# Attention mixers of a hybrid block: sparse-attention steps taken in pairs, and three work lists merged by how an item uses the TensorE array

## What is computed

```python
def dsa_mixer(q, k, v, q_idx, k_idx, w_idx, rel_bias_dsa):   # 4 heads of 64, one shared k and v
    def block(inp):                                          # 128 queries at a time
        ...
        _, sel = lax.top_k(score, n_sel)                     # done in an earlier stage, as a mask
        logits = jnp.einsum('bthd,btkd->bhtk', qb, kg).astype(f32)
        logits = jnp.where(valid[:, None], logits + bias, -jnp.inf)
        probs = jax.nn.softmax(logits, axis=-1).astype(vg.dtype)
        return jnp.einsum('bhtk,btkd->bthd', probs, vg)

def swa_mixer(q, k, v, sinks, rel_bias_swa):                 # 8 heads, window of 128
    logits = jnp.einsum('bnqhgd,bnkhd->bnhgqk', qb, kw).astype(f32) + bias.astype(f32)
    ...
    out = jnp.einsum('bnhgqk,bnkhd->bnqhgd', probs.astype(vw.dtype), vw)

def gla_mixer(q, k, v, g, a_lr, w_alpha2, b_alpha, g_norm):  # gated linear attention, chunks of 64
    def step(state, inp):
        o = o_inter + jnp.einsum('bhts,bhsv->bhtv', scores, vi)
        state = (jnp.exp(b_last[:, :, 0, :])[..., None] * state
                 + jnp.einsum('bhsk,bhsv->bhkv', ki * jnp.exp(b_last - bi), vi))
```

## Time and profile before

| what | value |
|---|---|
| three runs | 2830.13, 2831.82, 2831.91 us |
| median | 2831.82 us |
| profiled execution, span from first to last instruction | 2830.9 us |
| outside the span, against the median | 0.9 us |
| mixers: first instruction after the stage's start, last copy out issued | about 845 us, 1357.15 us |
| mixers, PE / DVE / ACT busy in 845 to 1357 us | 441.9 / 393.3 / 343.2 of 512 us |

### The profile page before, as it was taken

The page is one execution under the profiler, slowest core; times in us unless marked ns, Lnnn a source line. Parts: engine busy times, 40 slices in busy tenths (PEclk is TensorE's granted clock), DMA queues, the critical chain, the costliest instruction groups (busy, mean ns, idle before and its releaser), DMA issues. The chain is left out here.

```text
span 2830.9 us, 34992 instructions
## 1 busy us (share of the span) xinstructions
PE 2596.2 (92%) x10908; PEld 1642.9 (58%) x10909; DVE 1813.7 (64%) x2566; ACT 1283.1 (45%) x2400; POOL 922.8 (33%) x925
## 2 busy tenths in 40 slices
PE   6988779999987899898799979999999999998998
PEld 3634323344863445444688756666666666665787
DVE  2176999699977788876333486644644444743676
ACT  2277867967956676766321222222222222222322
POOL 2377877700011111121000043434444444433221
PEclk9999989999997899999899989999999999999999
DMA  5101131113152123222544459975776665973663
GB/s 151 63 33 42 32 58 38 35 63 98 38 169 78 62 73 102 76 71 74 200 143 143 177 224 356 351 273 210 282 270 227 237 223 201 347 286 138 198 216 132
DMA packets 221474, 438.08 MB, mean 155 GB/s; under 512 B 22888, under 2 KB 91048, under 8 KB 221224
## 3 DMA queue, kind: packets, MB, share of 16 engines
q1 hardware_dynamic: 199400, 357.78, 36.8%
q0 software_dynamic: 13312, 47.32, 5.3%
q10 hardware_dynamic: 8640, 31.46, 2.7%
HBM read 331.14 MB, written 105.38 MB: 154 GB/s over the span
## 5 line engine op out<-in xcount | busy, mean ns | idle before, releaser
L2504 DVE CAST p_high<-p_low 128x2048 fp32r<-128x2048 f32 x128 | 203.0, 1586 | 400.4 <-PE p_psG L2611 293.3
L698 PE MATMUL p_psP<-home,p_ring 128*128 128x512 f32 x832 | 366.3, 598 | 0.0
L2627 PE MATMUL p_psY<-p_wd,p_hT 128*128 x752 | 330.9, 593 | 2.4 <-ACT p_hT L2686 2.2
L2506 DVE TENSOR_TENSOR p_low<-p_low,p_high 128x2048 fp32r<-128x2048 f32 x128 | 318.9, 2492 | 4.4
L698 PEld LDWEIGHTS p_psP<-home,p_ring 128*128 128x128 f32 x832 | 157.3, 191 | 205.0 <-issue 204.9
L2627 PEld LDWEIGHTS p_psY<-p_wd,p_hT 128*128 128x128 f32 x752 | 139.3, 190 | 160.6 <-issue 160.4
L727 PE MATMUL p_psI<-p_kI,p_qI 64*128 64x512 f32 (+3 forms) x608 | 148.1, 596 | 62.9 <-ACT p_relu L589 62.8
L2547 POOL TENSOR_TENSOR p_xT_low<-p_xT,p_xT_high 128x512 fp32r<-128x512 f32 x94 | 186.1, 1998 | 3.4 <-ACT p_xT L2671 3.4
L2609 PE MATMUL p_psG<-p_high,p_xT_high 128*128 128x512 f32 x376 | 167.2, 445 | 15.8 <-DVE p_low L2506 8.2
L2553 POOL TENSOR_TENSOR p_hid<-p_act_g,p_act_u 128x512 f32<-128x512 f32 x47 | 62.2, 1324 | 307.7 <-ACT p_act_u L2681 294.8
L603 ACT ACTIVATE p_relu<-p_relu,p_small 128x512 f32<-128x512 f32 (+3 forms) x266 | 161.5, 662 | 0.0
(11 more groups left out here) (423 smaller groups left out, 5833.4 us busy)
## 6 DMA issues: line engine op xcount, KB each, us to landing
p_low<-in_w_expert_gate_dram SPq DMA_DIRECT2D x32, 2048.0 KB, 13.5
p_low<-in_w_expert_up_dram SPq DMA_DIRECT2D x32, 2048.0 KB, 18.3
p_wd<-in_w_expert_down_dram SPq DMA_DIRECT2D x32, 2048.0 KB, 10.7
y_dram<-p_y ACTq DMA_DIRECT2D x47, 512.0 KB, 8.1
p_xt<-in_x_dram SPq DMA_DIRECT2D x32, 512.0 KB, 4.7
y_dram<-p_clear SPq DMA_DIRECT2D x32, 512.0 KB, 4.3
proj_f<-p_stage SPq DMA_DIRECT2D x52, 256.0 KB, 2.4
p_ot<-o_dram SPq DMA_DIRECT2D x16, 512.0 KB, 4.5
```

Source lines behind the costliest of these rows:

```text
L698: mm = pe.matmul(psP[0:n, i % 2, :], w, aT[:, k, c * CH:(c + 1) * CH], start=k == 0, stop=k == KD - 1)
L2504: dve.tensor_copy(high[:, m, k, :], low[:, par, m, k, :].bitcast(F32)).then_inc(high_done, 1)
L2506: dve.tensor_tensor(low[:, par, m, k, :], low[:, par, m, k, :].bitcast(F32), high[:, m, k, :].bitcast(F32), ALU.subtract).then_inc(w_split, 1)
L2627: mm = pe.matmul(psY[:, c, :], hT[:, k, :], wd[:, bass.ds(at, 1), k, c * CH:(c + 1) * CH].rearrange("p a f -> p (a f)"), start=k == 0, sto ...
```

## The change

`stream_a` now takes the steps of a pass in pairs (passes with more than two steps): two T items, then the Q items due in both, then the two V items that the lag lets through. The slots advance by the same sum. And the three streams are no longer sorted by time: `merged` looks at the heads of the three streams that are due within 1.0 slot of the earliest and takes the first whose mode equals that of the item before; items that use no array count as alike. Nothing is added to or taken from the work of any item.

```diff
--- before.py
+++ after.py
@@ -1118,21 +1118,22 @@
             n, ahead, at = steps_of(u), [], 0
             if u + 1 < NU:
                 ahead = [("Q", u + 1, ci) for ci in range(len(chunks(block_of(u + 1))))]
-            for sp in range(n):
-                slot += 1 + 1.5 / n
+            for sp in range(0, n, 2 if n > 2 else 1):
+                both_now = range(sp, min(sp + 2, n)) if n > 2 else range(sp, sp + 1)
+                slot += (1 + 1.5 / n) * len(both_now)
                 now = []
                 if sp == 0:
                     at = len(ahead) if n <= 2 else min(1, len(ahead))
                     now += ahead[:at]
-                now.append(("T", u, sp))
+                now += [("T", u, s) for s in both_now]
 
                 while behind and behind[0][0] == "O":
                     now.append(behind.pop(0))
-                upto = max(at, min(len(ahead), -(-len(ahead) * (sp + 1) * 2 // n)))
+                upto = max(at, min(len(ahead), -(-len(ahead) * (both_now[-1] + 1) * 2 // n)))
                 now += ahead[at:upto]
                 at = upto
-                behind.append(("V", u, sp))
-                if sp == n - 1:
+                behind += [("V", u, s) for s in both_now]
+                if n - 1 in both_now:
                     behind += [("P", u), ("O", u)]
 
                 while sum(b[0] == "V" for b in behind) > 2:
@@ -1140,7 +1141,7 @@
                 while behind[0][0] == "P":
                     now.append(behind.pop(0))
                 if u + 1 < NU:
-                    now += [("E", u + 1, h) for h in range(2) if sp == max(0, n - 3 + h)]
+                    now += [("E", u + 1, h) for h in range(2) if max(0, n - 3 + h) in both_now]
                 stream_a += now
                 a_step += [slot] * len(now)
         stream_a += behind
@@ -1175,7 +1176,24 @@
             return [(first + (end - first) * i / len(stream), item) for i, item in enumerate(stream)]
         timed = [(t, 0, item) for t, item in zip(a_step, stream_a)]
         timed += [(t, 1, item) for t, item in spread(stream_w, 0.3, W_END * slots)] + [(t, 2, item) for t, item in spread(stream_g, 0.6, G_END * slots)]
-        items = [item for _, _, item in sorted(timed, key=lambda x: x[:2])]
+        tiled = {"Q": "rows", "q": "rows", "u": "rows", "T": "whole", "t": "whole", "O": "whole", "o": "whole", "a": "whole", "s": "whole", "V": "columns", "v": "columns"}
+
+        def merged(timed):
+
+            heads, at = [[(t, item) for t, k, item in timed if k == stream] for stream in range(3)], [0, 0, 0]
+            out, mode = [], None
+            while any(at[k] < len(heads[k]) for k in range(3)):
+                there = sorted((heads[k][at[k]][0], k) for k in range(3) if at[k] < len(heads[k]))
+                near = [k for t, k in there if t <= there[0][0] + 1.0]
+                alike = [k for k in near if tiled.get(heads[k][at[k]][1][0], mode) == mode]
+                k = (alike or near)[0]
+                item = heads[k][at[k]][1]
+                mode = "columns" if item[0] == "w" else tiled.get(item[0], mode)
+                out.append(item)
+                at[k] += 1
+            return out
+
+        items = merged(timed)
 
 
         l_use, x_use, x_behind = {}, {}, {}
```

## The result

| | before | the change |
|---|---|---|
| median of four runs | 2831.86 us | 2842.84 us |
| runs | 2830.13 to 2832.65 | 2841.72 to 2848.22 |
| ratio | | 1.0043 [1.0031, 1.0054] |
| profiled execution, span (its own time) | 2830.9 | 2840.4 (2842.16) |
| mixers, first to last weight load | 510.8 us | 520.3 us |

A forecast was written before the change was run, and what follows sets the result against it. PE was taken as fullest in the long middle, with DVE close. The span 2830.9 - 19.9 + 7.5 = 2818.5 us, with 0.9 us outside it, gave 2819.4 us; range 2806 to 2838.

The forecast's parts named there:

- Part 1: PE's issue order in the mixers: 172 fewer mode changes at 0.16 us each, 27.5 us of PE time saved.
- Part 2: Passes 8 to 31: PE's saving capped at half the idle time of DVE or ACT, so 19.9 us arrives.
- second rival: Neighbours DVE and ACT take the saving: 7.6 us gained, 7.5 lost to new waits, 2831.7 us, no change; chance 0.25.
- Part 3: Window attention: items pulled nearer their feeders make v wait 2.95 us and o 4.57 more, together 7.5 us.
- Pairing itself: T, T asks ACT for two copies before V; the wait was put at zero, covered by the pair before.
- Parting two Q: Concerns two Q in a row holding four of seven banks until DVE has read both; cost put at nothing.
- Third rival: Look-ahead puts copies behind ACT's exponentials at seven v and o places, 33 us of waits, 2844.9 us; chance 0.16.
- SP and POOL at zero: SP and POOL follow the same list; nothing ties PE to them, so their effect was taken as zero.
- the next stage one for one: The stage after starts with a wait for its own loads, so it shifts one for one with this stage's end.

The follow-up runs named there:

- e5: e1 with a pair's T and the Q ahead of its first V due one step earlier than that V; 2813.6 us, 0.9936 of before.
- e9: e1 with v, then o, moved later until three array items stand behind the item that feeds them; 2821.5 us, 0.9963 of before.
- e13: The kernel before, with v and o moved later until three array items stand behind their feeders; 2828.3 us, 0.9985 of before.
- e6: e1 with the second of two Q put behind the V pair (T T Q V V Q); 2832.6 us, 1.0004 of before.
- e1: The change with its pairs alone: the three lists sorted by due time again instead of merged by mode; 2838.5 us, 1.0023 of before.

## Why the prediction was wrong, step by step

- **Part 1, 172 changes at 0.16 us, 27.5 us**: right as far as it can be seen. The measured part is the pairs: most T pairs between other modes take 1.02 us in the changed trace (9 of 13) and most V pairs 1.01 (31 of 41), where 1.02 and 1.01 were forecast. That the hold fell by 27.0 us is a sum over prices of before and so confirms the count, not the price. The Trainium skill says, on the page "TensorEngine Tiling (Array Packing)", section "Key Properties", that changing the tiling mode drains TensorE; it gives no price. The traces agree, with 0.15 to 0.18 us for one.
- **Part 2, half of the neighbour's idle time, 19.9 of the 27.5 us**: not tested by the change, whose new waits hide it. e5 is the nearest test, with 128 changes fewer, 20.0 us of hold, and 18.3 us off the stage and off the median (the span of its profiled run is 22.3 us shorter, 4.0 of it outside the stage). By passes the limit did not come out: for the change it allowed 5.8 us in passes 8 to 15, 7.8 in 16 to 23 and 6.3 in 24 to 31, and e5 gained 6.3, 1.6 and 10.4. The second rival, with the Trainium skill's page "TensorEngine Tiling (Array Packing)", section "PSUM Bottleneck", behind it, asked for longer waits for DVE's reading. At Q and q, for DVE's reading of Q, these were 3.7 and 2.4 us in all in the changed kernel, so that rule did not make the change slow. In e5 all waits of PE for DVE's reading of q (p_lg) come to some 15 us, after 8 before, but in passes 16 to 23 they are 3.2 after 2.7. No run here shows that rule at work.
- **Part 3, what the merging adds, 7.5 us**: right in kind for v, too small, and put down to the wrong cause. v waits 11.9 us in 4 places, mean 3.0 and longest 4.4 us, against five at 0.59: the copy itself is short, but up to four exponentials stand before it. For o I had 4.57 us more, in blocks 5 and 9; by the wait view it has less than before, by the sums of rest 12.6 against 13.9, and its longest wait stands in block 14 as before.
- **"Pairing itself ... This wait is zero"**: the step that failed. I looked for T's copies and the banks, and asked only whether the pair's own items wait for each other. The cost was with the neighbours in the list: a shared due time changes what can stand between items of the other streams. The pairs alone cost 6.8 us where they should have given 19.0 by their hold: 25.8 us, and e5 gets 24.9 of it back. 13.7 to 17.1 us of it are v and o right behind their feeders (e9, e13). In the profiled runs the pairs bring 13.9 us more idle time of PE, and 13.2 us by which busy time fell less than hold, of which some 11 are the clock's. Parting two Q, also put at nothing, left the idle time as it was (e6).
- **Third rival, 2844.9 us**: it was within 2.1 us of the result, by a mechanism right in kind, but the closeness is luck. It had 33 us of new waits at v and o against 19.9 us of saving; by the wait view v and o together have 22.6 us after 13.7, and most of the 36.5 us of new rest stands elsewhere. It named the look-ahead as the source, and the look-ahead is the smaller one (4.3 us from e1 to the change).
- **SP and POOL at zero, the next stage one for one**: right for the stage behind it. Its first product, as in the earlier trace rows, starts 8.86 us later (1372.80 after 1363.94), after the same wait of 7.27 us:

```profile
1372.80 1.97 PE L2000 MATMUL p_psT<-ident,p_ot 128*128 128x128 f32 x8 [7.27 <-DMA p_ot<-o_dram]
```

- **The clock**: a term that the sum put at nothing without a word. In 960 to 1290 us the granted clock is 0.94 instead of 0.98, and over the stage PE has 84.6 us of busy time at 1.2 GHz instead of 61.8, some 10 of the 36.5 us of new rest.

What stays open is why the clock is low more often in some lists. It does not go by PE's idle time alone: e1 and e6 are idle for 83.2 and 83.5 us and have 85.3 and 67.0 us of busy time at 1.2 GHz. No edit here held the list and changed the clock, and each of these figures is of one execution. Open are also the part of the T waits that e9 leaves, and the banks, which every edit of the list gives out anew.

## What to carry to other kernels

Where one merged list sets the order on engines that run in order, grouping the items of one stream also moves what lies between the items of all others: after such a change list, for every feeder and its consumer, how many items stand between them, before pricing anything else. The count shows where to look, not what it costs: one item between was enough in some blocks here and not in others, by what the feeding engine was doing. When items are grouped, keep the due time that each had, so that other streams still fall between them. And compare a saving with what arrived part by part, and split what is missing into idle time and busy time at the lower clock: here the sum over the stage agreed within 2 us while two parts missed by 8 and by 5. A neighbour that is 93% busy cost PE 1.0 us of idle time in passes 16 to 23, so its share alone was no reason to cut the saving; the prediction had not looked at the clock, which fits nearly all of what is missing there.

## What the runs showed of the hardware

A change of mode cost about the same between all three uses of the array (rows, whole, columns): 0.15 us from a t and a T in a row, 0.15 from V and v, 0.18 from q and Q, all in the trace of before, and 0.15 and 0.16 from the pairs of T and of V in the changed kernel (1.03 and 1.01 us). In e1 and e5 most T pairs between other modes hold the array 1.02 us (20 and 19 of 27) and most V pairs 1.01. The loss of 25 us lay in the order of the list and not in this price.

Lists with equal work and equal idle time of PE can differ in the granted clock. e1 and e6 run the same items with 83.2 and 83.5 us of idle time; e6 has 18.3 us less busy time at 1.2 GHz, and its stage is 6.7 us shorter in the profiled run. At 1.2 GHz a V holds the array 1.05 us instead of 0.58, a Q of 512 keys 2.01 instead of 1.06.
